# Splitting the recurrence's output projection into three reduced-precision products, with single row buffers

## The reference, cut to what matters

```python
proj  = h @ w_in                                   # rows q,k,v,gate of both mixers
o_a = gated_delta_net(...)   # 4 heads of 128: chunked solve, state S_a
o_b = retention(...)         # 4 heads of 128: rope, decayed scores, state S_b
mixed = concat([o_a, o_b], -1)                     # (1024 tokens, 1024)
x = x + mixed @ w_out                              # the projection that changes
h2 = rms_norm(x, ffn_norm)
x = x + hierarchical_moe(h2, ...)                  # 64 experts, top 2
return rms_norm(x, final_norm)
```

## Time and profile before

| | |
|---|---|
| runs | 2123.18, 2123.31, 2125.99 us |
| median | 2123.31 us |
| span of the profiled execution | 2126.7 us |
| PE, DVE, ACT, POOL busy | 92%, 38%, 29%, 29% of the span |
| recurrence, first whole step to the first product of the experts | about 1188 to 1580 us |
| DMA in the experts' stage | 97% to 98% of 16 engines, some 405 GB/s |
| mean granted TensorE clock | 0.967 of full speed |

### The profile page before, as it was taken

One profiled execution on the slowest core, in us unless ns is written; L12 is line 12 of the kernel. 1 busy time (PEld: TensorE's weight loads), 2 busy tenths in 40 slices (PEclk: granted clock), 3 DMA queues, 4 the chain that ended last, 5 costly groups with the idle time before them and its releaser, 6 DMA issues. The chain is left out here.

```text
span 2126.7 us, 31150 instructions
## 1 busy us (share of the span) xinstructions
PE 1956.5 (92%) x12049; PEld 1379.7 (65%) x12049; DVE 808.6 (38%) x1461; ACT 615.9 (29%) x1324; POOL 606.6 (29%) x619
## 2 busy tenths in 40 slices
PE   8999999999999989999999899999979888888885
PEld 7998887787787767878887666666563222322222
DVE  5223256666453443440112456676531211111114
ACT  5333145555323432331112432232212111111111
POOL 1226387332211110010114676665211111111102
PEclk9999999999999999999999999999989989999998
DMA  5103461211420253622332422211659999999996
GB/s 208 52 31 140 147 200 26 51 26 46 150 83 28 45 122 67 83 60 94 94 119 86 161 83 95 81 56 55 260 224 417 425 424 425 423 422 420 418 383 263
DMA packets 101730, 371.80 MB, mean 175 GB/s; under 512 B 17429, under 2 KB 40154, under 8 KB 74714
## 3 DMA queue, kind: packets, MB, share of 16 engines
q1 hardware_dynamic: 82592, 323.55, 42.6%
q0 software_dynamic: 16704, 42.10, 5.1%
q10 hardware_dynamic: 2298, 4.23, 0.5%
HBM read 321.47 MB, written 65.14 MB: 182 GB/s over the span
## 5 line engine op out<-in xcount | busy, mean ns | idle before, releaser
L2907 PE MATMUL ps<-w_gu,rows_t 128*64 128x512 f32 x1024 | 260.4, 667 | 58.1 <-DMA w_gu<-w_up 56.5
L2907 PEld LDWEIGHTS ps<-w_gu,rows_t 128*64 128x64 f32 x1024 | 79.2, 152 | 216.1 <-issue 155.8
L3165 POOL DMA_INDIRECT y_d<-y_out,asg_i x32 | 32.2, 1006 | 429.9 <-DVE y_out L2991 414.7
L2982 DVE TENSOR_TENSOR act_s<-act_g,ps 128x256 f32<-128x256 f32 x32 | 13.5, 421 | 326.1 <-ACT act_g L2973 326.1
L2334 PE MATMUL ps<-w_o,mix_t 128*128 128x512 f32 x256 | 124.3, 616 | 0.0
L2925 PE MATMUL ps<-w_d,act_tt 128*64 128x512 f32 x512 | 116.9, 598 | 0.5 <-issue 0.5
L1120 ACT ACTIVATE prob<-ps,stats 128x1024 f32<-128x1024 f32 (+7 forms) x128 | 94.5, 738 | 62.1 <-DVE stats L1083 61.7
L2973 ACT ACTIVATE act_g<-ps 128x256 f32<-128x256 f32 x32 | 12.3, 384 | 323.7 <-PE ps L2907 323.7
L310 PE MATMUL ps<-tk_lo,h_hi 128*128 128x512 f32 x256 | 100.4, 392 | 3.0 <-DVE tk_lo L302 3.0
L310 PE MATMUL ps<-tk_hi,h_lo 128*128 128x512 f32 x256 | 100.3, 392 | 0.0
L310 PE MATMUL ps<-tk_hi,h_hi 128*128 128x512 f32 x256 | 100.2, 392 | 0.0
(11 more groups left out here) (477 smaller groups left out, 4389.6 us busy)
## 6 DMA issues: line engine op xcount, KB each, us to landing
w_gu<-w_gate SPq DMA_DIRECT2D x64, 1024.0 KB, 20.0
w_gu<-w_up SPq DMA_DIRECT2D x64, 1024.0 KB, 23.5
w_d<-w_down SPq DMA_DIRECT2D x64, 1024.0 KB, 23.6
w_tk<-w_in SPq DMA_DIRECT2D x5, 2048.0 KB, 13.6
proj_d<-tok_o POOLq DMA_DIRECT2D x40, 256.0 KB, 2.3
tk_in<-proj_d SPq DMA_DIRECT2D x8, 1280.0 KB, 5.9
w_ch<-w_in SPq DMA_DIRECT2D x12, 512.0 KB, 10.2
proj_d<-conv_o POOLq DMA_DIRECT2D x12, 512.0 KB, 3.9
```

Source lines behind the costliest of these rows:

```text
L2907: mm = pe.matmul(ps[half, 2, :].rearrange("p (g n) -> p g n", g=2), rows_t[:, k, half], w_gu[q][:, h, :, k, :], start=(k == 0), stop=(k == ...
L2982: v.tensor_tensor(act_s[:, :].rearrange("q (k p) -> q k p", k=2), by_k(act_g[:, :]), by_k(ps[:, 2, DE:]), ALU.mult).then_inc(s_acts, 1)
L3165: pool.indirect_dma_start(out=y_d, out_offset=bass.IndirectOffsetOnAxis(ap=idx, axis=0), in_=y_out[q][:, :], in_offset=None, bounds_check= ...
```

## The change

The projection of `mixed` by `w_out` is no longer one float32 product but three products of float32r parts: a high part (the value as ACT writes it in float32r) and a low part (the rest, by a subtraction on DVE). Of the first half of the columns, `e_p0` does the 16 products that need the high part of `mixed` only, `e_p1` the 8 with the low part. Of the second half each k of `OUT1` makes three products.

ACT makes `mix_hi` from M0 and M1 but no longer frees the banks; DVE makes `mix_lo` from the same banks in the new part of the piece `e_p0` (`mix_low`) and frees them. `HOME`, `ORDER` and `ENDING` are as before. ACT makes the high weights in place of the scaled ones; DVE makes the low weights in step 1, two of eight rows in each of `n_ut3` to `n_ut6`. The two scalings of QS and CR go from DVE to ACT, each as four instructions of 128 columns. The row buffers `qkv_in`, `tk_in` and `qk_r` become single; the rows of `tk_in` are loaded in two pieces (queries and keys; values and gates), each when its readers are through. `w_o2` comes in three DMAs after all stores of the projection. Tiles move in SBUF; the space that the software DMA queue keeps there is set to 4096 bytes, and all tiles start 12288 bytes lower. In step 8 only pair 0's gate and up weights are loaded, its down weights follow in step 9.

```diff
-        base_off = 16512
+        base_off = 4224
...
-        qkv_in = take("qkv_in", [P, 3 * NA], 2)
+        qkv_in = take("qkv_in", [P, 3 * NA])
...
             load_qkv(sp, 0)
-            load_qkv(sp, 1)
...
+            load_qkv(sp, 1)
+            load_qk(sp, 1)
             products_over(sp)
-            load_tk(sp, 1)
-            sp.dma_start(w_o2[:, :, :], ...).then_inc(s_wo2, 16)
+            for q in range(4):
+                wait(sp, s_tst[q], 16 * 10)
+            for (k, n, _), part in zip(W_LO, w_raw):
+                sp.dma_start(part[:, :, :], ...[:, k:k + n, :]).then_inc(s_wo2, 16)

         def load_qkv(sp, t):
+            dve_a.wait(sp, "qkn", t - 1)
+            pool_n.wait(sp, "vb", t - 1)
...
+        def load_qk(sp, t):
+            pool_n.wait(sp, "sinx", t - 1)
...
+        def load_vg(sp, t):
+            if t > 0:
+                full(sp, "SR", t - 1)
+                pool_o.wait(sp, "og", t - 1)
...
-            def project(t, j, ks):
...
+            def first_half_high(t):
+                act_e.wait(pe, "h0", t)
+                act_e.wait(pe, "h1", t)
+                pe.wait_ge(s_wos, KD)
+                pe.wait_ge(s_wol, WOL0 + KD)
+                b = begin(pe, "OUT0", t)
+                for k in range(KD):
+                    pe.matmul(b, mix_hi[:, k, :], w_part(w_low, k)[:, 0:BANK], start=(k == 0), stop=False)
+                    pe.matmul(b, mix_hi[:, k, :], w_hi[:, k, 0:BANK], start=False, stop=False)
+
+            def first_half_low(t):
+                copied(pe, "M0", t)
+                copied(pe, "M1", t)
+                b = ps[:, place["OUT0", t][0], :]
+                for k in range(KD):
+                    mm = pe.matmul(b, mix_lo[:, k, :], w_hi[:, k, 0:BANK], start=False, stop=(k == KD - 1))
+                filled(mm, "OUT0", t)
+
+            def second_half(ks):
...
+                    for k in ks:
+                        pe.matmul(b, mix_hi[:, k, :], w_part(w_low, k)[:, BANK:], start=(k == 0), stop=False)
+                        pe.matmul(b, mix_lo[:, k, :], w_hi[:, k, BANK:], start=False, stop=False)
+                        mm = pe.matmul(b, mix_hi[:, k, :], w_hi[:, k, BANK:], start=False, stop=(k == KD - 1))
...
+            def scaled(job, t, dst, scale):
+                b = read(act, job, t)
+                for h in range(4):
+                    ins = act.activation(dst[:, h, :], q4(b)[:, h, :], ACT.Copy, scale=scale[:, h:h + 1])
+                freed(ins, job, t)
+
+            def o_read(t):
+                pool_o.wait(act, "og", t - 1)
+                scaled("QS", t, o_cat[:, 0:4, :], gt(G_EGC, t))
+
+            def o_mix(t):
+                scaled("CR", t, o_cat[:, 4:8, :], const("qdec"))
...
             def e_turn(t):
-                copy("M0", t, mix_t[:, 0:4, :])
-                copy("M1", t, mix_t[:, 4:8, :])
+                for j in range(2):
+                    b = read(act, f"M{j}", t)
+                    act_e.done(act.activation(flat4(mix_hi[:, 4 * j:4 * j + 4, :]), b, ACT.Copy), f"h{j}")
...
+            def mix_low(t):
+                for j in range(2):
+                    act_e.wait(v, f"h{j}", t)
+                    b = read(v, f"M{j}", t)
+                    part = slice(4 * j, 4 * j + 4)
+                    freed(low(v, flat4(mix_lo[:, part, :]), b, flat4(mix_hi[:, part, :])), f"M{j}", t)
+
+            def low_weights(i, then):
...
+                    for k in (2 * i, 2 * i + 1):
+                        v.wait_ge(s_wos, k + 1)
+                        g = 0 if k < AH else 1 + k - AH
+                        v.scalar_tensor_tensor(w_part(w_low, k), w_part(w_raw, k), gain_ab[:, g:g + 1], w_hi[:, k, :].bitcast(F32),
+                                               ALU.mult, ALU.subtract).then_inc(s_wol, 1)
...
+                        full(pool, "TK", t - 1)
+                        pool_o.wait(pool, "kdk", t - 1)
...
-    nc = bacc.Bacc("TRN2", target_bir_lowering=False, num_devices=1)
+    nc = bacc.Bacc("TRN2", target_bir_lowering=False, num_devices=1, dynamic_dma_scratch_size=4096)
```

More of the change, by code:

```diff
@@ L1888, in build @@
         k_t0, q_t0 = take("k_t0", H4), take("q_t0", H4)
+        sin_x = take("sin_x", H8)
+        x_lev = take("x_lev", C4, 2)
         gate_rows = take("gate_rows", [P, 2, AH])
@@ L1892, in build @@
         u_fin0, attn_t0, v_b0, k_d20 = (take(x, H4) for x in ("u_fin0", "attn_t0", "v_b0", "k_d20"))
[L1893 removed]
+        qk_r = take("qk_r", H8)
         rot = take("rot", [P, T, HD])
         take = area(at(136), at(152))
[L1897 removed]
+        tk_in = take("tk_in", [P, 5, BANK])
         cos_x = take("cos_x", H8)
@@ L1906, in build, with w_part @@
         o_cat = take("o_cat", H8)
-        take = area(at(64), at(120))
-        w_o2 = take("w_o2", [P, KD, D])
-        mixed, mix_t = take("mixed", H8), take("mix_t", H8)
         s_a, s_ad = take("s_a", H4), take("s_ad", H4)
[L1913 to L1920, removed]
+        s_b, s_bd, k_dk, p_t = (take(x, H4) for x in ("s_b", "s_bd", "k_dk", "p_t"))
+        w_hi = sb("w_o2_hi", [P, KD, D], at(64), F32R)
+        W_LO = ((0, 4, at(96)), (4, 2, at(112)), (6, 2, at(152)))
+        w_raw = [sb(f"w_o2_raw{k}", [P, n, D], o) for k, n, o in W_LO]
+        w_low = [sb(f"w_o2_lo{k}", [P, n, D], o, F32R) for k, n, o in W_LO]
+        def w_part(parts, k):
+            i = 0 if k < 4 else 1 if k < 6 else 2
+            return parts[i][:, k - W_LO[i][0], :]
+        take = area(at(160), 229344 - base_off)
+        mixed = take("mixed", H8)
+        mix_hi, mix_lo = take("mix_hi", H8, dt=F32R), take("mix_lo", H8, dt=F32R)
+        qb_t, kb_t = take("qb_t", H4), take("kb_t", H4)
         hn_t = take("hn_t", H8)
         fg_row = take("fg_row", [P, D])
+        hn = take("hn", [P, D])
+        res2 = take("res2_", [P, D], 2)
         w_r = take("w_r", [P, KD, NL])
@@ L2310, in o_mix @@
             def o_mix(t):
-                vals = q4(tk_in[t % 2][:, 3, :])
+                vals = q4(tk_in[:, 3, :])
                 copied(pe, "SB", t)
-                loaded(pe, s_ldB, t)
+                rows_loaded(pe, s_ldV, t)
                 four("IN", t, p_t, vals)
@@ L2378, in d_pe @@
                 pieces[f"n_ut{s}"] = level_ut(s)
-            for i in range(8):
-                pieces[f"e_p{i}"] = lambda t, i=i: project(t, int(i > 1), range(4 * i, 4 * i + 4) if i < 2 else OUT1[i])
+            pieces["e_p0"], pieces["e_p1"] = first_half_high, first_half_low
+            for i in range(2, 8):
+                pieces[f"e_p{i}"] = second_half(OUT1[i])
             own = {f"k{i}": lambda i=i: last_product(pe, i) for i in range(3 * T)}
@@ L2398, in a_sums @@
             def a_sums(t):
-                loaded(act, s_ldA, t)
+                rows_loaded(act, s_ldA, t)
                 pool_a.wait(act, "ms", t - 1)
                 pool_n.wait(act, "rot", t - 1)
-                act_a.done(head_squares(sin_x, lambda h: qkv_in[t % 2][:, h * HD:(h + 1) * HD], ss_qk), "sq")
+                act_a.done(head_squares(sin_x, lambda h: qkv_in[:, h * HD:(h + 1) * HD], ss_qk), "sq")
             def n_turn(t):
@@ L2490, in a_norm @@
                 pool_a.wait(v, "rsq", t)
-                loaded(v, s_ldA, t)
+                rows_loaded(v, s_ldA, t)
                 full(v, "KT", t - 1)
                 pool_n.wait(v, "kd", t - 1)
-                dve_a.done(v.tensor_tensor(qk_n[:, :, :], qkv_in[t % 2][:, 0:2 * NA].rearrange("p (h n) -> p h n", h=8),
+                dve_a.done(v.tensor_tensor(qk_n[:, :, :], qkv_in[:, 0:2 * NA].rearrange("p (h n) -> p h n", h=8),
                                            bc(rs_qk, HD), ALU.mult), "qkn")
@@ L2546, in o_read @@
                 dve_o.done(v.tensor_tensor(rhs[:, :, :], rhs[:, :, :], v_b[t % 2][:, :, :], ALU.add), "r")
-                b = read(v, "QS", t)
-                freed(v.tensor_tensor(o_cat[:, 0:4, :], q4(b), bc(gt(G_EGC, t), HD), ALU.mult), "QS", t)
             def o_out(t):
@@ L2562, in o_mix @@
             def o_mix(t):
-                b = read(v, "CR", t)
-                freed(v.tensor_tensor(o_cat[:, 4:8, :], q4(b), bc(const("qdec"), HD), ALU.mult), "CR", t)
                 copied(v, "CR", t)
@@ L2717, in n_first @@
                 x_level(1, t)
-                vals = q4(qkv_in[t % 2][:, 2 * NA:])
-                loaded(pool, s_ldA, t)
+                vals = q4(qkv_in[:, 2 * NA:])
+                rows_loaded(pool, s_ldA, t)
                 pool_n.done(tt(v_b[t % 2][:, :, :], vals, bc(gt(G_BETA, t), HD), ALU.mult), "vb")
@@ L2725, in by_table @@
                     wait(pool, s_wr, 48)
-                x = tk_in[t % 2][:, 1:3, :].rearrange("p a (h n) -> p (a h) n", n=half)
+                x = tk_in[:, 1:3, :].rearrange("p a (h n) -> p (a h) n", n=half)
                 pool_n.done(tt(dst[:, :, :].rearrange("p h (a n) -> p (h a) n", a=2), x,
@@ L2759, in o_sq @@
             def o_sq(t):
-                if t == 0:
-                    for q in range(4):
-                        wait(pool, s_tst[q], 16 * 10)
```

97 lines of the change are left out of this document (49 added, 48 removed).

## The result

The changed kernel takes 2163.84 us, the median of four runs (2162.81 to 2167.33), against 2124.16 us before (four runs, 2123.18 to 2125.99). The ratio is 1.0188, 95% interval 1.0174 to 1.0202: 1.9% slower, some 40 us. The forecast was 2146 us, slower, with a range to 2162; the direction came, and the loss is larger (40 us and not 23) and lies 2 us beyond the range. The profiled execution has a span of 2165.6 us (2126.7 before), and the mean granted clock is 0.955 (0.967).

A forecast was written before the change was run, and what follows sets the result against it. PE was taken to set each recurrence step, with the experts' weight stream passing changes through. Steps 3 to 7 +12.0, step 8 +1.3, step 9 -1.3, step 2 0, step 1 +3, clock +8: +23, 2146 us, range 2128 to 2162.

The forecast's parts named there:

- What bounds it: PE sets the recurrence step (busy 43.31 of 46.50 us); the experts' weight stream passes recurrence changes on one to one.
- Products, -2.6: Projection by w_out: float32r parts take 12.5 us a block against 15.1 in float32, a gain of 2.6.
- Wait at `e_p0`, 4.2: PE waits 4.2 us (3.4 to 4.6) in step 4 for bank 6, freed by mix_low behind n_scores and l_hn.
- Clock, 1.7 us a wait: Behind six waits in steps 3 to 8, 3.4 us at half clock loses 1.7 us each; taken as +8 us.
- +25: Upper end of the sum if, by the skill's rule, all six waits are followed by slow work; +15 without it.
- Lost cover, 0.8: In the inverse, PE's waits for DVE's updates grow as pieces between them shrink: 0.8 us a step (0 to 1.0).
- DVE's lost scaling of CR: in step 4 DVE had been waiting for PE there: Moving CR's scaling off DVE was costed at nothing, as DVE had been waiting for PE there.
- Step 1, +3, and step 2, 0: Step 1: making and later landing of weights, +3 us (0 to +8). Step 2: waits and product gain, about 0.
- Pair 0's down weights, 2 MB in step 9, are wanted some 70 us later: Loading these weights in step 9 was costed at nothing, as their reader comes much later.
- The smaller queue space, 0: The smaller space of the software DMA queue was costed at nothing: no row shows it full.
- Single buffers, `tk_in` in parts, SP's waits: Costed at nothing: qkv_in's reload has 7 us spare, tk_in loads over 10 us early, SP holds only later-needed DMAs.
- Rival 2: mix_low is done before PE needs bank 6: -12, 2111 us, faster; gains below 1.8 us wait a step; chance 0.08.

The follow-up runs named there:

- b_idle: The changed kernel with 28 idle PE transposes ahead of the products of e_p0 in steps 2 to 7: 2151.25 us, ratio 1.0135 to the kernel before.
- c_four: The changed kernel with mixed's low parts ahead of l_hn, CR and QS scaled by DVE, pair 0's down weights ahead of pair 2: 2115.96 us, ratio 0.9953.
- a2_crback: The changed kernel with only the scaling of CR given back to DVE: 2150.71 us, ratio 1.0120 to the kernel before.
- c_sums: The changed kernel with a_sums moved ahead of o_mix, ACT still scaling CR: 2151.18 us, ratio 1.0116 to the kernel before.
- c_four_nolow: c_four with DVE's low-weight operations on 64 of 1024 columns and PE reading high weights in place of low ones: 2109.85 us, ratio 0.9922.
- b_act: The kernel before with the scaled copies of QS and CR moved to ACT and nothing else: 2132.44 us, ratio 1.0042.
- b_three: The changed kernel with mixed's low parts ahead of l_hn, CR scaled by DVE, pair 0's down weights ahead of pair 2: 2125.33 us, ratio 1.0006.
- a1_early: The changed kernel with DVE's low parts of mixed ahead of l_hn in steps 1 to 8: 2136.75 us, ratio 1.0061 to the kernel before.

## Why the prediction was right and wrong

- **What bounds it**: right. The experts' stage kept its wait for weights (56.4 us), and losses went through, less 2.9 us, which is within its scatter.
- **Products, -2.6**: right (-2.5).
- **Wait at `e_p0`, 4.2**: right in kind, place and cause, 3.44 in size, the lower end of its range. The queue was the one described; ACT's four copies took 1.1 us and not 0.8. Measured from the step's start, the bank was free at 13.2 us and not at 11.3, but PE too came later, at 9.8 and not at 7.1, 2.0 us of it by the waits for `tri_g` and `k_t`.
- **Clock, 1.7 us a wait**: mis-sized. The stretch behind each of the six waits of steps 3 to 8 was one of 6.8 us at half clock, not 3.4, lying nearly whole in work: 2.8 us a step by b_idle, 12.6 us in all and not 8. The row of 10.2 us in the earlier trace rows had shown that stretches can be longer. The sentence that PE's longest wait from 1229.6 to 1529.9 was 1.2 us is also misread: one of 1.89 us ends at 1528.28, and from 1529.6 the clock is at half for 3.4 us. The rule of the Trainium skill in TensorE: Matmul & The Clock Gate, section Why this matters for your kernels, that idle gaps between bursts bring the half rate back, agrees with the trace: all six waits of 3.4 to 3.5 us were followed by it, and some of 2.0 us were too (below). Its sum, +25, was nearer than +23 but still too small, as it priced the short stretch.
- **Lost cover, 0.8**: wrong in form. In steps 3 to 7 of after the updates' waits went and did not grow; other waits came. With those gone too, in c_four, what PE waits for outside `e_p0` is 0.4 us less than before.
- **"DVE's lost scaling of CR: in step 4 DVE had been waiting for PE there"**: the step that failed most. It looked at the engine that lost the work and not at the queue that took it. ACT, in order, stands for CR ahead of `a_sums`, and POOL's chain to `tri_g` had 4 us to spare against a shift of 4 us and a step whose PE work had shrunk: PE waits 2.0 us a step for `tri_g` and `k_t`. With CR's scaling back on DVE 13 us go (a2_crback), and as much with `a_sums` ahead of it (c_sums). The term stood at nothing and was the largest that the sum lacked.
- **Step 1, +3, and step 2, 0**: the low weights cost 3.5 in step 1 (c_four_nolow). ACT's scaled copies, named there without a price, cost 4.1 in the same step (b_act). In after the step took 6.4 more, less than the two costs added, and the half-clock stretch that was 10.2 us from 1219.4 is now 17.1 from 1220.8. Step 2 has the forecast wait of 2.0 at `e_p0`, but 1.8 us more for `tri_g` and a half-clock stretch of 3.4 us, neither forecast. Step 8 took 4.7 us more and not 2.6.
- **"Pair 0's down weights, 2 MB in step 9, are wanted some 70 us later"**: true of the weights, and no answer: 6.1 us came from what they pushed aside, the store of `hn`.
- **The smaller queue space, 0**: a gain of 3.5 us, at the end of the program and not in the stream.
- **Single buffers, `tk_in` in parts, SP's waits**: PE's and POOL's waits show no load of rows in steps 2 to 7. Right, as far as the traces tell; no run tests it alone.

These costs overlap (b_three), so they don't add up to the 17 us between forecast and loss; c_four, which takes back ACT's copies, the order of two pieces and the down weights, is 48 us below after.

Rival 2 named the cure: with the low parts early, the wait was 1.5 us, under its point of 1.8. There it said the change gains, at 2111 us, and a1_early is at 2137, still 0.6% slower than before, by the terms above. Its 27 us for the waits and a1_early's 27 us agree by luck: the rival took all waits away and counted the clock's 8 on top, while a1_early leaves 1.5 us of each wait and by b_idle 12 to 13 of its 27 us are the clock.

Left open: what sets the length of a slow stretch, and how the store of `hn` loses 5.7 us in the queues.

## What to carry to other kernels

When work moves from one engine to another, price it at the place in the receiving queue: list what stands behind it there, in every step that has a different load, and follow that to the next reader with no slack. When a transfer moves, ask what shares the queues with it at that moment, not when its own reader comes. And when an accumulator's bank is handed over by another engine, put that engine's release ahead of any long operation that nobody waits for.

## What was not expected of the hardware

- POOL's last drain took 9.3 us with the default queue space and 3.1 or 2.2 us with 4096 bytes.
- The half-clock stretch behind a wait at `e_p0` was 6.8 us in steps 3 to 8 of after (waits of 3.4 to 3.5), and 3.4 or 6.8 in a2_crback and c_sums (waits of 3.7 to 4.0). With waits of 2.0 us two of steps 4 to 7 of b_three had one, and so had step 2 of after (3.4 us each). With 1.5 in steps 3 to 8 of a1_early there was none, and with 1.4 in c_four none either (its one slow stretch in steps 3 to 7, from 1401.4, lies at the end of step 5).
- `hn` on DVE took 2.04 us in after and 2.70 in a1_early, beside other work of POOL; the earlier trace rows have 1.28 for the like form. The Trainium skill, in SBUF — State Buffer, section SBUF: two separate sides, says that a DVE operation with two SBUF inputs and a GpSimd operation keep each other out of a shared port. The traces fit: two `x_lev` of POOL beside `hn` took 3.20 us in after, and 1.41 in a1_early, where `hn` comes later. `tri_g` beside the low weights, 4.39 us and not 1.04, has the same form; no run tests the port by itself.
